# Selections of the sparse attention spread over blocks 0-1, 2-3, 4-5 and 6, and the mixer's split, the first variance and two low parts put into block 7

## The reference

```
h = x @ w_in                         # projections of all heads
out_a = u * (w_s @ layer_norm(v))    # mixer, 4 groups
# differential attention, 4 heads, each with two softmaxes
attn = p[:, :, 0] - lam * p[:, :, 1];  out_b = rms_norm(attn @ v)
# sparse attention, 4 heads: only the 256 keys with the highest score
score = sum_h(w_h * relu(q_h @ k));  sel = top_k(score, 256)
out_c = softmax(q @ k[sel] * scale - slope * dist) @ v[sel]
x = layer_norm(alpha * x + concat(out_a, out_b, out_c) @ w_out)
```

## Time and profile before

| | us |
|---|---|
| median of 3 runs | 2191.62 |
| lowest and highest | 2189.8 and 2192.68 |
| the profiled execution | 2190.99 |
| its span in the profile | 2189.2 |
| PE busy | 2123.0 |
| DVE busy | 1093.3 |
| ACT busy | 748.0 |
| POOL busy | 177.9 |

### The profile page before, as it was taken

One profiled execution on the slowest core, in us unless ns is written; L12 is line 12 of the kernel. 1 busy time (PEld: TensorE's weight loads), 2 busy tenths in 40 slices (PEclk: granted clock), 3 DMA queues, 4 the chain that ended last, 5 costly groups with the idle time before them and its releaser, 6 DMA issues.

```text
span 2189.2 us, 25882 instructions
## 1 busy us (share of the span) xinstructions
PE 2123.0 (97%) x9838; PEld 1692.5 (77%) x9838; DVE 1093.3 (50%) x1703; ACT 748.0 (34%) x1191; POOL 177.9 (8%) x159
## 2 busy tenths in 40 slices
PE   7999999999999999999979998999999999999998
PEld 3888888878888887688856667878788888888877
DVE  6744463663324373888897664483412222222136
ACT  4311124431112443665755654242111111111133
POOL 1000002300000231102210000310000000000000
PEclk9999999999999999999977999999999999999999
DMA  8532333222111422101110002221111111111141
GB/s 300 165 116 87 100 107 91 77 68 67 48 48 48 125 81 87 58 13 39 49 30 1 1 1 106 87 77 53 53 48 47 44 57 50 42 48 58 46 127 77
DMA packets 222092, 154.75 MB, mean 71 GB/s; under 512 B 6565, under 2 KB 209462, under 8 KB 221878
## 3 DMA queue, kind: packets, MB, share of 16 engines
q1 hardware_dynamic: 215392, 134.53, 20.2%
q0 software_dynamic: 4608, 16.78, 2.4%
q10 hardware_dynamic: 2006, 2.31, 0.3%
HBM read 145.21 MB, written 8.39 MB: 70 GB/s over the span
## 4 chain that ended last, share of the span: by engine, by line
PE 84%; DVE 7%; ACT 5%; issue 2%; SPq 1%; DMA 1%; POOL 0%; DVEq 0%; ACTq 0%; POOLq 0%
PE pair L2146 36%; PE pair L2163 18%; PE pair L2596 8%; PE pair L2349 3%; PE pair L2483 3%; PE pair L2204 3%; PE pair L2451 2%; ACT proj L1003 2%; PE pair L2382 1%; PE pair L2666 1%; PE pair L2465 1%; PE pair L2370 1%; PE pair L2175 1%; SPq L519 1%; DVE w_lo L1332 1%
## 5 line engine op out<-in xcount | busy, mean ns | idle before, releaser
L1338 DVE TENSOR_TENSOR w_lo<-w_raw,w_hi 128x1024 fp32r<-128x1024 f32 x101 | 123.8, 1225 | 673.4 <-ACT w_hi L782 673.1
L782 ACT ACTIVATE w_hi<-w_raw 128x1024 fp32r<-128x1024 f32 x102 | 108.2, 1061 | 804.1 <-PE pair L2146 623.0
L2146 PE MATMUL pair<-act_hi,w_hi 128*128 128x512 f32 x1168 | 361.2, 391 | 1.8 <-ACT v_all L943 1.8
L2146 PE MATMUL pair<-act_lo,w_hi 128*128 128x512 f32 x1168 | 359.7, 389 | 0.0
L2146 PE MATMUL pair<-act_hi,w_lo 128*128 128x512 f32 x1168 | 359.7, 389 | 0.0
L2146 PEld LDWEIGHTS pair<-act_hi,w_hi 128*128 128x128 f32 x1168 | 218.9, 188 | 48.8 <-ACT v_all L943 2.2
L2146 PEld LDWEIGHTS pair<-act_hi,w_lo 128*128 128x128 f32 x1168 | 219.2, 188 | 45.8
L2146 PEld LDWEIGHTS pair<-act_lo,w_hi 128*128 128x128 f32 x1168 | 219.2, 188 | 45.6
L2163 PE MATMUL pair<-act_hi,w_hi 128*128 128x512 f32 x608 | 244.3, 402 | 3.8 <-DVE act_lo L1351 2.0
L2163 PE MATMUL pair<-act_hi,w_lo 128*128 128x512 f32 x608 | 238.1, 392 | 0.0
L2163 PE MATMUL pair<-act_lo,w_hi 128*128 128x512 f32 x608 | 238.1, 392 | 0.0
(11 more groups left out here) (416 smaller groups left out, 3151.3 us busy)
## 6 DMA issues: line engine op xcount, KB each, us to landing
w_raw<-w_in SPq DMA_DIRECT2D x76, 512.0 KB, 3.8
w_raw<-w_out SPq DMA_DIRECT2D x48, 512.0 KB, 3.9
w_raw<-w_gu SPq DMA_DIRECT2D x48, 512.0 KB, 3.8
w_raw<-w_down SPq DMA_DIRECT2D x24, 384.0 KB, 3.1
act_region<-w_ada SPq DMA_DIRECT2D x16, 512.0 KB, 13.8
sq<-w_ada POOLq DMA_DIRECT2D x16, 512.0 KB, 4.2
sq_sum<-w_ada POOLq DMA_DIRECT2D x16, 512.0 KB, 4.8
yT<-x SPq DMA_DIRECT2D x8, 512.0 KB, 7.1
```

What stands on the lines that cost most here:

```text
L782: A(w_hi[s_][:], w_raw[s_][:], ACT.Copy).then_inc(hi_ready, 1)
L1338: v.tensor_tensor(w_lo[s_][:], w_raw[s_][:], f32(w_hi[s_][:]), ALU.subtract)\
L2146: i = mm(bank[pair][:, h * HALF:(h + 1) * HALF], w[slot][:, k, :], a[:, k, h * HALF:(h + 1) * HALF], start=(k == 0 and w is w_hi and a is ...
```

## The change

- The selection of tile 4 starts at item 2, of tile 5 at item 13, of tile 6 at item 29 and of tile 7 at item 36, each a step an item. Tiles 2 and 3 stay.
- The marks of equal keys are kept in row 0 of `act_region` and no longer in the projection row that holds the mixer's output.
- ACT's four high parts of the mixer's output move from the loop's start into the first four items of block 7, behind a wait for all selections. DVE's low parts follow two items later.
- The variance, root and scaling of blocks 0 to 3 move from block 4 to the same items of block 7.
- ACT writes the high part of unit 15 after the last projection's copy instead of before it.
- POOL makes the low parts of units 14 and 15 once the sparse output of block 6 is taken. DVE's wait for them moves behind the loop.

```diff
+SELECT_FROM = {4: 2, 5: 13, 6: 29, 7: 36}
...
-            for n in range(5, N_UNITS + 2):
+            for n in range(5, N_UNITS):
+                unit_lo(n)
+            pool.wait_ge(c_taken, TT - 1)
+            for n in range(N_UNITS, N_UNITS + 2):
                 unit_lo(n)
...
             for n in range(2, N_UNITS):
-                unit_hi(n + 2)
+                if n < N_UNITS - 1:
+                    unit_hi(n + 2)
+                else:
+                    act.wait_ge(unit_done, 1 + U_PROJ + n + 2)
...
+            unit_hi(N_UNITS + 1)
...
             exps(0)
-            for b in range(2):
-                for a in range(2):
-                    A(act_hi[:, b, a * HALF:(a + 1) * HALF], proj[:, S_AU + b, a * HALF:(a + 1) * HALF], ACT.Copy)\
-                        .then_inc(s_hi, 1)
...
-                if k == 4 * ITEMS + 2:
+                if i == TT - 1 and it < MIX_CHUNKS:
+                    b, a = divmod(it, 2)
+                    act.wait_ge(sel_done, N_TS)
+                    A(act_hi[:, b, a * HALF:(a + 1) * HALF], proj[:, S_AU + b, a * HALF:(a + 1) * HALF], ACT.Copy)\
+                        .then_inc(s_hi, 1)
+                if k == 7 * ITEMS + 2:
                     act.wait_ge(ob_var, 1)
...
-                same = junk[:, 0:n] if i in EARLY_SEL else proj[:, S_AU, 0:n]
+                same = junk[:, 0:n] if i in EARLY_SEL else act_region[:, 0, 0:n]
...
-                if SEL0 + len(EARLY_SEL) + i < TT:
-                    select(SEL0 + len(EARLY_SEL) + i, it)
-                if k < MIX_CHUNKS:
-                    b, a = divmod(k, 2)
-                    dve.wait_ge(s_hi, SP_MIX + k + 1)
+                for s_, at in SELECT_FROM.items():
+                    if at <= k < at + 6:
+                        select(s_, k - at)
+                if i == TT - 1 and it >= 2:
+                    b, a = divmod(it - 2, 2)
+                    dve.wait_ge(s_hi, SP_MIX + it - 1)
...
-                if k == MIX_CHUNKS:
-                    dve.wait_ge(pool_lo, N_UNITS + 2)
-                    dve.sem_inc(lo_ready, N_UNITS + 2)
...
-                if k == 4 * ITEMS + 1:
+                if k == 7 * ITEMS + 1:
                     ob_variance(0)
-                if k == 4 * ITEMS + 4:
+                if k == 7 * ITEMS + 4:
                     ob_scale(0)
+            dve.wait_ge(pool_lo, N_UNITS + 2)
+            dve.sem_inc(lo_ready, N_UNITS + 2)
```

## The result

The changed kernel took 2179.33 us in the median of four executions (2176.58 to 2183.36), the kernel before 2192.15 in the same comparison (four, 2189.8 to 2194.49): ratio 0.9935, interval 0.9916 to 0.9954, so 12.8 us faster. A second set of four (the first experiment) had a median of 2177.0 and a ratio of 0.9949 (0.9932 to 0.9965). The forecast was 2174.0, or -17.6 us.

What follows compares the result with a forecast made beforehand. TensorE was busy for 97% of the span; in the attention loop DVE bound blocks 0 to 3 and PE blocks 5 and 6. The terms summed to -17.6 us, 2174.0 against the median of 2191.62, range 2167 to 2184.

Steps and rivals of the forecast that it cites:

- start: Start of the attention loop: earlier projection and POOL's parts gone bring the first probability copy sooner, -3.3 us.
- block 0: Attention loop: counting, is-equal, scan and three low parts leave DVE, two steps of tile 4 enter; -2.8 us.
- block 1: Attention loop: selection passes leave DVE's differential items, two passes of 0.8 to 0.9 enter; -1.5 us.
- block 2: Attention loop: selection passes leave DVE's differential items, net 2.3, the first 0.7 in a wait for PE; -1.6 us.
- block 3, with 7.0 for the clock: Attention loop: DVE's selection passes leave, -2.2 us, and the sparse items run at full clock, 7.0 us less.
- block 4, with 1.3 for the clock: Attention loop: variance and square root leave, -1.4 us, and the rest of the low-clock stretch goes, 1.3 us.
- blocks 5 and 6: Late attention blocks: five steps of tile 6 and all of tile 7 move in, mostly into DVE's rest; +1.0 us.
- block 7: Last attention block: variance, scaling, low parts and POOL's two passes +1.9 us, root work with ACT's copies +0.6.
- The clock term: Block 3 into block 4: the fall of TensorE's clock at 1191.4 us goes; -8.3 us, bounds 0 and 8.3.
- Rival 2: Low-clock stretches of blocks 1 and 2 shrink also, PE being less starved: 3.5 us more, 2170.5 us; chance 0.18.
- The root's term: Block 7: variance and square root from block 4, with ACT's act_hi copies ahead, find longer items; +0.6 us.
- Rivals 3 and 4: 3: DVE's work only carried to other blocks, 2196 us, chance 0.05; 4: clock stays low until block 4, 2197.3, 0.04.

Runs made afterwards that it cites:

- the first experiment: The changed kernel run again with no edit; median 2177.0 us, ratio 0.9949.
- without spreading: The changed kernel, but tiles 4 to 7 are selected in blocks 0 to 3 as before; median 2191.96 us of ten, ratio 1.0005.
- tile 7 alone moved: The changed kernel, but tiles 4 to 6 are selected as before and only tile 7 in block 6; median 2185.16 us of ten, ratio 0.9984.
- spreading alone: The kernel before with only the places of the selections of tiles 4 to 7 changed; median 2180.69 us of five, ratio 0.9963.
- all three together: Changed kernel: scans in sparse items, POOL after last combine, block 7's variance, root and scaling later, last low part before second scaling; 2173.29 us, ratio 0.9914.
- The experiment with the steps moved: The changed kernel with tile 6 selected from item 25 and tile 7 from item 31; 2177.86 us, ratio 0.9936.
- the two experiments that move POOL: The changed kernel with POOL's low parts at their old place, 2176.75 us, or begun after the loop's last combine, 2176.87 us, ratio 0.9931.
- its own experiment: The changed kernel with ACT's root at item 4 and DVE's scaling at item 5 of block 7; 2176.20 us, ratio 0.9926.

## Why the prediction held in part

Direction and range were right; the forecast was 5.3 us too low against the first median, 3.0 against the second. By its own steps:

| step | forecast | the change less before, profiles |
|---|---|---|
| start | -3.3 | -3.2 |
| block 0 | -2.8 | -2.2 |
| block 1 | -1.5 | -5.8 |
| block 2 | -1.6 | -1.2 |
| block 3, with 7.0 for the clock | -9.2 | -9.0 |
| block 4, with 1.3 for the clock | -2.7 | -2.3 |
| blocks 5 and 6 | +1.0 | +3.1 |
| block 7 | +2.5 | +2.7 |

**The clock term** failed: "I expect the fall at 1191.4 to go" booked 8.3 us as if the kernel before always paid them. It pays them in some executions. The price itself was near: the sparse items of block 3 take 4.76 + 5.46 = 10.2 us at the full clock, as estimated, and the block 24.51 instead of 31.50, 7.0 us less. Only the rest in block 4 was set too high, 0.45 us (30.09 against 29.64) and not 1.3; so the fall costs 7.4 us for 20.5 us at the low level. Against the second profile of before the loop's gain is 3.2 + 2.1 + 6.1 + 1.2 + 2.0 + 1.9 - 1.5 - 1.6 - 2.6 = 10.8 us, not 17.9. The mechanism behind it (the gap lets the clock fall) is half right. The gap is there in all four profiles with tile 7 in block 3, the fall in one; in the ten without that selection there block 3 ran at the full clock each time. One of four against none of ten is too little to show it for block 3; for block 1 five of five against none of nine does show that the fall hangs on the selections' places.

**Rival 2** was no alternative but happened too. The fall of block 1 goes with tile 5's selection, 14 profiles of 14. That is why block 1 gave 5.8 where 1.5 was booked: its two sparse items, which had run at half clock, went from 4.55 + 5.24 to 3.02 + 3.19 us. That is 3.6 us, about the 3.5 at which the rival was priced; two passes of tile 5's selection left them too, and what part of the 3.6 is theirs isn't shown.

How do these two come to -13 in the median? The mean granted clock is on record for all executions in the table, profiled or not. A share of low time s lowers it by s/2, so 0.001 is 4.4 us more at the low level. This agrees with the profiles: without spreading, the low stretches of the first profile add up to 60 us, and its clock is 0.986.

| kernel | executions | median us | median clock | lowest and highest clock |
|---|---|---|---|---|
| before | 40 | 2190.7 | 0.983 | 0.979, 0.986 |
| without spreading | 11 | 2191.4 | 0.982 | 0.978, 0.986 |
| tile 7 alone moved | 10 | 2185.2 | 0.985 | 0.982, 0.989 |
| spreading alone | 5 | 2180.7 | 0.988 | 0.987, 0.989 |
| the change | 8 | 2177.6 | 0.989 | 0.986, 0.990 |
| all three together | 6 | 2173.3 | 0.988 | 0.988, 0.992 |

A line through the 40 executions of before gives 1.59 us for each 0.001 of clock (give or take 0.27), 0.36 us for each us at the low level. The fall in block 3 gives the same, 7.4 / 20.5. The step from 0.983 to 0.989 is 26 us less at the low level, or 6 x 1.59 = 9.5 of the 13.1 us between the medians. So the clock did give about what was booked, mostly at another place: the two profiles of before against the two of the change show 13.7 of those 26 us in block 1 and 3.4 to 6.8 at the loop's start (23.9 us low, now 20.5 and 17.1). Nothing was booked for either. That the total came within 3 to 5 us of the forecast is in part luck: block 1's fall made up for one in block 3 that comes only at times.

The profile of the kernel without spreading, at 0.986 against a median of 0.982, was a lucky one: most of its executions have some 17 us more at the low level, worth 6 us. This also tells why moving tile 7 gives 6.2 to 6.8 us in the medians and 0.6 between two profiles: 0.003 of clock, 13 us at the low level, are 4.8. That those 13 us lie in block 3 is likely, not shown; the unprofiled executions have no traces.

What is left for all other steps is 3.6 us by the same line. The profiles say 6.9: the start, blocks 0, 2 and 4 give 3.2 + 2.2 + 1.2 + 1.9, block 3 at the full clock 2.0, and block 1's differential items 2.2 (10.28 to 8.05, with some of the clock in it), less 5.8 late. The difference of 3.3 stays open; the third digit of the two clocks alone leaves room for 1.6 of it. It lies mostly with the edits other than the spreading: by the profiles they give 3.9 us at the full clock (start 3.2, block 0 1.4, block 4 1.9, less 2.6 in block 7), while the kernel without spreading has a median 0.7 above that of before at 0.001 less clock, a gain of only 0.9.

**Blocks 5 and 6** failed at "Only the scans exceed that": 1.8 and 2.0 us of rest an item are means over six, and the sparse items hold more than their share. In block 6 the item with the count (1.28 us) grew from 5.61 to 6.56 and that with the scan from 3.60 to 4.12; in block 5 the scan's from 4.74 to 5.69. The experiment with the steps moved takes 2.1 us of the 3.1 off, and puts 0.9 on block 4.

**Block 7** held, with the root's term set somewhat low. The timeline of the change shows POOL's two passes back to back and what they met:

```profile
1282.91 4.70 POOL L698 TENSOR_TENSOR w_lo<-w_raw,w_hi 128x1024 fp32r<-128x1024 f32 x2 [182.19 <-DVE params_wpool L1748]
...
1284.19 0.75 DVE L1725 CUSTOM_DVE_ANT_0 act_region<-pair,buf_a,neg_max 128x512 f32<-128x512 f32 x1
...
1285.73 1.90 DVE L1737 SCALAR_TENSOR_TENSOR den_r<-den,den_r,lam 128x1 f32<-128x1 f32 x1
...
1287.66 1.28 DVE L1739 SCALAR_TENSOR_TENSOR act_region<-act_region,den_r 128x1024 f32<-128x1024 f32 x1
...
1289.00 1.09 PE L2474 MATMUL pair<-identity,act_region 128*128 128x128 f32 x8 [0.53 <-DVE act_region L1739]
...
1291.25 0.73 PE L2456 MATMUL pair<-sel_bias,one_id 128*128 128x512 f32 x2 [0.94 <-DVE neg_max L1725]
```

An operation on 128 x 1 elements, 0.22 us elsewhere, began at 1285.73 and ended when POOL did. It met the second pass, and the combine took 1.90 + 1.28 = 3.2 us, as forecast. On this bears the Trainium skill (SBUF — State Buffer, Who interferes with whom): a DVE instruction that reads both inputs from SBUF shares a port pair with GpSimd, and one holds it against the other for its whole length. The 1.90 agrees, and so does the pass at 1284.19, which has an input in PSUM and took its usual 0.75 under POOL. So the engines of this kernel don't wait for each other on semaphores only, as was said at the start: no semaphore stands between POOL's pass and this operation. Of the two passes one held something up: 1.7 us by the two experiments that move POOL, where 1.9 with the variance was booked. With POOL away the variance costs 6.40 - 6.28 = 0.1.

The root's term was +0.6 and is 0.9 by its own experiment. ACT's rows in the change, and the product on PE that waited for the copy:

```profile
1299.44 1.28 ACT L1097 ACT_TABLE_LOAD   x1
...
1300.73 0.22 ACT L1097 ACTIVATE o_ss<-o_ss 128x16 f32<-128x16 f32 x1
...
1300.97 1.28 ACT L1061 ACT_TABLE_LOAD   x1
...
1304.54 1.00 ACT L1071 ACTIVATE act_region<-pair 128x1024 f32<-128x1024 f32 x1
...
1305.59 2.05 PE L2492 MATMUL pair<-v_all,act_region 128*128 128x128 f32 x16 [1.97 <-ACT act_region L1071]
```

In block 4 the same work cost 1.87 (29.64 against 27.77), where 1.4 was booked.

**Rivals 3 and 4**: the late blocks pay 5.8 us of the 25.5 that rival 3 needed in full, and in every profile the low stretch at the loop's start ended in block 1 at the latest.

## What to carry to other kernels

Where the clock is part of a gain, book the low stretch by how often it comes and not by the one profile that shows it: profile the kernel before twice, and read the mean clock of every execution. DVE work moved into a block that PE bounds is free only in the items that have the rest, so take the rest by item and not as a mean. Don't price a pass by its length alone: here a scan of 2.28 us put in by itself cost 0.09 us, and the whole selection with that scan 2.0.

## What the hardware showed beside

- Identical instructions after an identical PE gap fell to the low level in one execution and not in another: 1.74 of 3.40 us busy in block 3 (one of four profiles), 1.53 of 3.40 in block 2 (one of three). What decides it, these runs don't show.
- Low stretches at the program's start lasted 10.2 us in the first profile of before and 17.1 in its second, where the loop's first copy came 5.3 us later (1125.04 against 1119.75); the second also had the two stretches of 3.4 us at 476 and 923 us. The 13.7 us more at the low level are worth 4.9 by the line above. Single executions at a clock of 0.992 and 0.993 took 2165.88 and 2168.85 us, 7 us under the medians of their kernels.
- A table load and a root in the midst of exponentials cost 1.28 + 0.22 + 1.28 us, and the next activation began at once (1302.26). The Trainium skill (ScalarE: Activation LUTs, What ACT_TABLE_LOAD costs) gives about 1283 ns for the load and 1380 ns more for a drain at each switch; the load agrees, and of the drain these rows show nothing.
